# Root and scaling of a gated unit moved ahead of an attention, and an expert layer's gathers split by halves of the features

## What is computed

```
def even_mixer(h_lat, h_ctx, ...):
    ...
    o_lat = window_attention(q_lat, k_lat, v_lat, k_ctx, v_ctx, sink_g, scale)
    s_lat = spatial_gating(z_lat[..., EVEN_CTX_COLS + A_Q_W:], sgu_norm_g, sgu_w, sgu_b)
    y_lat = jnp.concatenate([o_lat, s_lat], axis=-1) @ w_out
    ...

def expert_choice_ffn(h, w_router, w1, w3, w2):
    n_tok, d = h.shape[1], h.shape[2]
    cap = EC_FACTOR * n_tok // N_EXPERTS
    aff = jax.nn.softmax(jnp.einsum('bnd,de->bne', h, w_router).astype(jnp.float32), axis=-1)
    gate, idx = lax.top_k(jnp.swapaxes(aff, 1, 2), cap)
    xs = jax.vmap(lambda hb, ib: hb[ib])(h, idx)
    a = jnp.einsum('becd,edf->becf', xs, w1)
    b = jnp.einsum('becd,edf->becf', xs, w3)
    y = jnp.einsum('becf,efd->becd', jax.nn.silu(a) * b, w2) * gate[..., None].astype(h.dtype)
    ...
```

## Time and profile before

| | us |
|---|---|
| median of 3 runs | 2015.21 |
| lowest, highest | 2009.55, 2015.6 |
| the profiled execution | 2012.53 |
| its span, first to last instruction | 2010.8 |
| PE busy | 1721.9 (86%) |
| DVE busy | 639.9 (32%) |
| ACT busy | 319.0 (16%) |
| HBM read | 580.11 MB |

### The profile page before, as it was taken

The page is one execution under the profiler, slowest core; times in us unless marked ns, Lnnn a source line. Parts: engine busy times, 40 slices in busy tenths (PEclk is TensorE's granted clock), DMA queues, the critical chain, the costliest instruction groups (busy, mean ns, idle before and its releaser), DMA issues.

```text
span 2010.8 us, 23441 instructions
## 1 busy us (share of the span) xinstructions
PE 1721.9 (86%) x10154; PEld 1059.0 (53%) x10154; DVE 639.9 (32%) x1276; ACT 319.0 (16%) x665; POOL 70.7 (4%) x82
## 2 busy tenths in 40 slices
PE   7999999999999998989999878889998765556565
PEld 4557588888888646464433222247577432222223
DVE  2885245688752047131111111121333100000002
ACT  4101231100101125021110000021242100000001
POOL 0000321000000000000000000000140000000000
PEclk8999999999999999989999999999999987887887
DMA  9679324776635022139999999992333999999995
GB/s 408 255 313 386 137 84 172 290 279 264 255 143 230 1 105 120 74 120 394 423 429 428 429 427 427 428 427 110 126 121 141 427 427 426 428 427 427 428 427 227
DMA packets 42437, 582.66 MB, mean 290 GB/s; under 512 B 4704, under 2 KB 4960, under 8 KB 6240
## 3 DMA queue, kind: packets, MB, share of 16 engines
q1 hardware_dynamic: 42336, 581.18, 69.9%
HBM read 580.11 MB, written 1.05 MB: 289 GB/s over the span
## 4 chain that ended last, share of the span: by engine, by line
PE 61%; DMA 30%; DVE 5%; ACT 2%; issue 1%; SPq 0%; DVEq 0%; POOL 0%; ACTq 0%
PE banks L652 38%; DMA ring<-in_experts_dram 29%; PE banks L1272 8%; PE banks L1295 4%; PE banks L1149 3%; PE banks L952 1%; DMA ring<-in_weights_dram 1%; PE banks L637 1%; PE banks L998 1%; PE banks L561 1%; DVE ring L1965 1%; PE banks L1021 1%; DVE small L2415 1%; PE banks L612 0%; PE banks L624 0%
## 5 line engine op out<-in xcount | busy, mean ns | idle before, releaser
L1272 PE MATMUL banks<-ring,arena 128*32 128x256 f32 (+1 forms) x2992 | 389.0, 524 | 164.8 <-DMA ring<-in_experts_dram 161.1
L652 PE MATMUL banks<-hT,ring 128*128 128x256 f32 (+2 forms) x1776 | 405.7, 389 | 6.5 <-ACT hT L1554 5.2
L652 PEld LDWEIGHTS banks<-hT,ring 128*128 128x128 f32 (+1 forms) x1776 | 333.9, 189 | 77.1 <-issue 31.6
L1272 PEld LDWEIGHTS banks<-ring,arena 128*32 128x32 f32 (+1 forms) x2992 | 143.3, 135 | 407.7 <-DMA ring<-in_experts_dram 220.4
L1965 DVE SCALAR_TENSOR_TENSOR ring<-ring,sil_c 128x512 f32<-128x512 f32 x336 | 242.6, 750 | 7.9
L1295 PE MATMUL banks<-ring,arena 128*32 128x256 f32 (+1 forms) x1536 | 186.9, 490 | 61.1 <-DMA ring<-in_experts_dram 38.9
L2617 DVE TENSOR_TENSOR arena<-arena,banks 128x512 f32<-128x512 f32 (+1 forms) x32 | 17.7, 555 | 524.1 <-PE banks L1272 524.1
L1295 PEld LDWEIGHTS banks<-ring,arena 128*32 128x32 f32 (+1 forms) x1536 | 70.0, 126 | 160.4 <-issue 77.4
L652 PE MATMUL banks<-arena,ring 128*128 128x256 f32 (+2 forms) x720 | 151.2, 371 | 2.7 <-POOL arena L2752 1.6
L652 PE MATMUL banks<-ring,hT 128*128 128x512 f32 (+1 forms) x384 | 147.0, 541 | 2.1 <-DVE arena L2174 2.1
L652 PEld LDWEIGHTS banks<-arena,ring 128*128 128x128 f32 (+1 forms) x720 | 130.6, 188 | 23.6 <-issue 2.6
(11 more groups left out here) (322 smaller groups left out, 1203.8 us busy)
## 6 DMA issues: line engine op xcount, KB each, us to landing
ring<-in_experts_dram SPq DMA_DIRECT2D x189, 2048.0 KB, 30.5
ring<-in_weights_dram SPq DMA_DIRECT2D x73, 2048.0 KB, 12.1
ring<-in_weights_dram SPq DMA_DIRECT2D x8, 1408.0 KB, 7.8
arena<-in_experts_dram SPq DMA_DIRECT2D x2, 2048.0 KB, 8.0
ring<-in_weights_dram SPq DMA_DIRECT2D x2, 1152.0 KB, 26.5
cT<-in_ctx_dram SPq DMA_DIRECT2D x2, 1024.0 KB, 7.5
ring<-in_weights_dram SPq DMA_DIRECT2D x2, 1024.0 KB, 15.4
ring<-in_weights_dram SPq DMA_DIRECT2D x1, 1536.0 KB, 28.3
```

What stands on the lines that cost most here:

```text
L652: ins = mm(dst, a, b, start=(i == 0), stop=(i == len(terms) - 1))
L1272: ins = mm(banks[M * q:M * q + M, which, 0:W], xc[:, 4 * half + k, :], w[k][:, W * q:W * q + W], start=(half == 0 and k == 0), stop=(half ...
```

## The change

On ACT the root moves from behind `eu3` to behind `eu0`, into the loop. On DVE `sgu_scaled()` moves from behind tile 2 of the attention to behind `sgu_variance()`, ahead of the attention. In `routed` three token tiles instead of four (layer 0), one instead of two (layer 1), are turned ahead of the affinities. The gather jobs go by a first and by stream second, and those with a = 1 take banks of the second rotation. `experts` waits at its start for the jobs with a = 0 only, and for those with a = 1 ahead of the second half of expert 0's w1.

```diff
--- before.py
+++ after.py
@@ -1167,7 +1167,7 @@
                         ins = mm(o[:, n:n + 17], router_part[s][:, P * c:P * c + P],
                                  const[:, C_RT + 17 * s:C_RT + 17 * s + 17], start=True, stop=True)
                 ins.then_inc(*jobs.fills(job))
-                half = TC * len(streams)
+                half = (3, 1)[l]
                 token_tiles = [(s, c, a) for s in streams for c in range(TC) for a in range(2)]
                 for s, c, a in token_tiles[:half]:
                     tokens_turned(l, s, c, a)
@@ -1181,12 +1181,13 @@
                 if jobs.new(f"mk{l}") > 1:
                     eng.wait_ge(*jobs.is_free(f"mk{l}"))
                 turn(f"mk{l}", [(48 * c, mk[0:48, P * c:P * c + P]) for c in range(TC)]).then_inc(*jobs.fills(f"mk{l}"))
-                for s in streams:
-                    for c in range(TC):
-                        eng.wait_ge(*jobs.is_drained(f"th{l}{s}{c}0"))
-                        eng.wait_ge(*jobs.is_drained(f"th{l}{s}{c}1"))
-                    eng.wait_ge(flag("selection"), sum(len(q) for q in ([0, 1], [0])[:l]) + s + 1)
-                    for a in range(2):
+                for a in range(2):
+                    for s in streams:
+                        if a == 0:
+                            for c in range(TC):
+                                eng.wait_ge(*jobs.is_drained(f"th{l}{s}{c}0"))
+                                eng.wait_ge(*jobs.is_drained(f"th{l}{s}{c}1"))
+                            eng.wait_ge(flag("selection"), sum(len(q) for q in ([0, 1], [0])[:l]) + s + 1)
                         gather_four(l, s, 0, a)
 
             def gather(l, s, half, kk):
@@ -1205,7 +1206,7 @@
             def gather_four(l, s, quarter, a):
 
                 job = f"gq{l}{s}{quarter}{a}"
-                if jobs.new(job, late=(quarter == 1)) > 1:
+                if jobs.new(job, late=(quarter == 1 or a == 1)) > 1:
                     eng.wait_ge(*jobs.is_free(job))
                 o = jobs.bank(job)
                 project([(o[:, P * j:P * j + P],
@@ -1244,8 +1245,7 @@
                 for b in range(4):
                     eng.wait_ge(drained[b], jobs.turns[b])
                 for s in streams:
-                    for a in range(2):
-                        eng.wait_ge(*jobs.is_drained(f"gq{l}{s}0{a}"))
+                    eng.wait_ge(*jobs.is_drained(f"gq{l}{s}00"))
                 for e in range(E):
                     n = E * l + e + 1
 
@@ -1267,6 +1267,9 @@
                     xc = x_slots(l)[:, e]
                     for which in range(2):
                         for half, w in stage_in(which):
+                            if e + which == 0 and half == 1:
+                                for s in streams:
+                                    eng.wait_ge(*jobs.is_drained(f"gq{l}{s}01"))
                             for k in range(4):
                                 for q in range(G):
                                     ins = mm(banks[M * q:M * q + M, which, 0:W], xc[:, 4 * half + k, :],
@@ -1786,9 +1789,10 @@
                 eng.wait_ge(*jobs.is_filled(f"eu{c}"))
                 o = jobs.bank(f"eu{c}")
                 A(e_u[:, c, :], o[:, :], ACT.Gelu_apprx_tanh).then_inc(*act.frees(f"eu{c}"))
-            eng.wait_ge(flag("sgu_var"), 1)
-            eng.wait_ge(*act.last)
-            A(lnst[:, :, 2], lnst[:, :, 2], ACT.Sqrt, scale=1.0 / 512, bias=eps).then_inc(*act.raises("sgu_std"))
+                if c == 0:
+                    eng.wait_ge(flag("sgu_var"), 1)
+                    eng.wait_ge(*act.last)
+                    A(lnst[:, :, 2], lnst[:, :, 2], ACT.Sqrt, scale=1.0 / 512, bias=eps).then_inc(*act.raises("sgu_std"))
             attention("ea", EVEN_TILES, e_p, e_pT, 64.0 ** -0.5, True)
             def routed(l, streams, residuals):
                 ns = len(streams)
@@ -2430,8 +2434,6 @@
                             TT(a[:, 4:6], a[:, 4:6], a[:, 6:8], ALU.add).then_inc(*dve.steps())
                         eng.wait_ge(*dve.last)
                         V.reciprocal(a[:, 0:2], a[:, 4:6]).then_inc(*dve.raises(f"reciprocal_{tag}"))
-                    if tag == "ea" and i == 2:
-                        sgu_scaled()
 
             gains(0, 1, 0, 1, V_M1)
             scale_shift("e1", 0, xT, 1, 0, "h3_0_v")
@@ -2461,6 +2463,7 @@
             for a in range(2):
                 rope_sum(f"esw{a + 1}", e_q[:, 2 * a:2 * a + 2, 0:N], 2, a + 2, "even")
             sgu_variance()
+            sgu_scaled()
             eng.wait_ge(*dve.last)
             TS(neg_sink, sink, -1.0, None, ALU.mult).then_inc(*dve.steps())
             attention("ea", EVEN_TILES, 64.0 ** -0.5,
```

## The result

The kernel after takes **1999.95 us**, the median of 6 executions (1998.51 to 2005.7), beside 2010.76 for the kernel before (6 executions, 2007.88 to 2015.6): ratio 0.9947, 95% interval 0.993 to 0.9963. That is 10.8 us less (7.4 to 14.1 by the interval). Run once more beside other runs of before (median 2011.36) it gave 2000.44 and 0.9943 [0.9927, 0.9959]. The forecast was 2005.0 with a range from 2000.5 to 2010.5: the sign is right, the saving nearly so (9.5 in the sum, 10.8 measured), the forecast time lies 5.05 us above the measured median, and that median lies 0.55 us under the range.

The account below looks back on a forecast made before the run. TensorE carries most of the chain, expert weights' transfers 29%; the first freed slot sets each expert stage's end. Terms 3.4 + 1.7 + 1.8 + 3.1 - 0.5 = 9.5 us: 2003.0 by profile, 2005.7 by median, forecast 2005, range 2000.5 to 2010.5.

Parts of the forecast that it names:

- part 1: Gated unit: root hidden on ACT, scaling moved off DVE between attention tiles 2 and 3; 3.4 us gain, bounds 2.4 to 5.8.
- part 4: Layer 1's routing: both gather jobs share bank 6, so the second waits; 0.5 us loss, bounds -2.8 to +2.8.
- A: Rival: the clock gives nothing back in layer 0, saving 6.4 us, time 2006 to 2009; chance 0.20.
- B: Rival: layer 1's bank collision costs its full 2.8 us, attention gives only 2.4; 2008 to 2011; chance 0.14.
- Rival D: Slower: even attention's tiles 5 to 15 run at half clock, over about 22 us; up to 2022; chance 0.03.
- the prediction's 0: Gated unit on ACT: moving the root and its table loads gains 0 and costs 0, being hidden.
- Part 2: Layer 0's routing: three token tiles ahead of the affinities start these earlier; 1.7 us gain, bounds 0.8 to 1.7.
- Part 3: Layer 0's gathers by halves: the hole ahead of expert 0 goes; 1.8 us gain, bounds 1.5 to 1.8.
- The clock of layer 0's gathers: TensorE's hole before layer 0's gathers halves to 1.5 us, so they run at full clock; 3.1 us gain, bounds 0 to 3.1.
- C: Rival: something else holds tile 3, the split wait doesn't bind, only tile order acts, 1.7 us; 2011 to 2015; chance 0.09.
- The fixed distance: Both layers' expert stages end a fixed distance behind the first freed weight slot, so whatever precedes it counts in full.

Follow-up runs that it names:

- experiment 5: Kernel before with only ScalarE's root moved behind the first Gelu, VectorE's scaling left in place: 2010.76 us, ratio 1.0001.
- experiments 1 to 3: Kernel before with one piece each: gated unit's root and scaling 2004.03 us; token-tile order 2007.96; gathers by halves with late banks and split wait 2008.3.
- experiment 7: Kernel before plus unread identity products on TensorE ahead of the chosen slots, 6 in layer 0 and 11 in layer 1: 2009.49 us, ratio 0.9994.
- experiment 8: Kernel after, layer 1's second gather on its own bank, plus 8 idle products between halves of expert 0's first projection in both layers: 1998.38 us, ratio 0.9947.
- experiment 9: Kernel after run again unchanged, in more rounds: 2000.44 us, ratio 0.9943 against the kernel before.
- experiment 11: Kernel after, layer 1's second gather on its own bank, plus idle products ahead of both layers' chosen slots and the odd attention's output sums: 1992.79 us, ratio 0.9908.
- experiment 10: Kernel after with layer 1's second gather job on bank 7 instead of bank 6: 1998.17 us, ratio 0.9932 against the kernel before.

## Why the prediction was right or wrong, point by point

- **The step that failed is the last one, from the sum to the forecast.** The sum was 9.5 us against the profiled 2012.53, 2003.0. I then went up by 2.0, to 2005, because the median of three executions lay 2.7 above the profiled one, at 2015.2. Over the 78 executions of the kernel before that ran beside the experiments the median is 2011.4 (2004.1 to 2019.7), so the time of the profiled execution was nearly ordinary (its clock, 0.946 where the 78 have 0.951 in the mean, was not), and two of the three were high ones. The correction had the wrong sign. Of the 5.05 us between 2005 and 1999.95, 2.0 are this correction, 1.8 the place of the profiled 2012.53 above the 2010.76 of before in the comparison, and 1.3 the sum itself (9.5 where 10.8 were measured). Sum against this level: 2001.9, measured 1999.95 and 2000.44.
- **The range was too narrow below** for the same reason: I let it end at 2000.5, above 2003.0 less what the bounds of the single terms allowed (up to 2.4 more for part 1 alone, 3.3 more for part 4). The text gave it as holding the forecast, A and most of B; it made no room for the high side of the terms.
- **Part 1**, term 3.4, bounds 2.4 to 5.8. The mechanism is right in each point: ScalarE's side 0 (experiment 5), VectorE's 3.46. What follows at tiles 4 and 5 brought more: over the whole attention the eight kernels with both moves have 86.46 to 87.63, mean 87.0, and the five with the scaling at its old place (before, 2, 3, 5, 7) 91.09 to 91.84, mean 91.3. So 4.3 is the size, 5.4 between the two first profiles, and the 3.4 was mis-sized by 0.9: with the scaling gone the attention was also granted the full clock more often (half clock for 0 to 3.4 us in the eight, 3.4 to 10.2 in the five). Rival D, which had it at half clock for more than 22 us, fell.
- **On the table loads** the Trainium skill ("ScalarE: Activation LUTs", section What ACT_TABLE_LOAD costs) puts 1283 ns and a drain of some 1380 ns to every switch to a different set of functions. The rows of after show the load of 1.28, but the root starts 0.04 us behind it, and two switches with the root take 2.92 us where by the Trainium skill the switches alone would take 5.3 (an estimate from its two figures). The measurement decides, and with it the prediction's 0.
- **Part 2**, term 1.7, bounds 0.8 to 1.7: 1.2 by the means and 0.7 to 1.0 at equal clock, so the term belonged at the lower end of its bounds. The 4.0 between the two first profiles is this and the luck of the clock.
- **Part 3**, term 1.8: about 1.9 in every kernel with the split. As forecast.
- **The clock of layer 0's gathers**, term 3.1 ("I take it whole"): the argument fell. Without added products the gathers lasted 10.24, 7.38, 9.01, 9.01 and 7.38 with the old order (mean 8.6), and 9.01, 9.01 and five times 7.38 with the new (mean 7.85). That is 0.8 in the mean, and not certain with so few. I had taken the one profile of before for the rule, when it was the worst of five, and I had derived from the length of one hole what the clock would do. The hole was wrong too: it is 2.2 to 2.3 us in every kernel with the new order, not 1.5, because the fourth token tile now stands behind the affinities, which I had left out when I let the tiles end where they did.
- **Part 4**, term -0.5, bounds -2.8 to +2.8: the double use of bank 6, its stop (1.46, forecast 1.4) and who ends it (VectorE) came as said; -0.2 in the mean, -0.7 in the first pair. The distance was 7.95, forecast 6.4 to 8.2. Rival B's form of it, a full price of 2.8, did not come. The other bound was mis-sized: by the prediction's own times a full clock would give back 7.23 less 1.8, 1.36, 0.1 and 1.8, that is 2.2 and not 2.8. The Trainium skill ("TensorE: Matmul & The Clock Gate", section A second HAM failure mode: psum-queue depth-cycling) has short stops between groups on banks make the clock swing; here the stretch with the stop ran at 0.50, but so did it before without one, so no run here shows that the stop did it.
- **Rivals A and C.** A, that the clock gives nothing back in layer 0's gathers, came closer than the forecast's term on that one point (0.8 of 3.1), but its time of 2006 to 2009 was too high: it had 6.4 us in all where 10.8 were measured, and it carried the same correction of 2.7. C fell with experiments 1 to 3.
- **The fixed distance** held in layer 1 (437.8 to 440.0) and was put on the wrong ground in layer 0 (experiment 8), without harm to the sum.

By means the terms are 4.3 + 1.2 + 1.9 + 0.8 - 0.2 = 8.0 us; measured are 10.8 and 10.9. The sum is inside the interval (7.4 to 14.1). That the recorded 9.5 came nearer is luck: it had the gathers' clock 2.3 too high and part 2 0.5 too high, and part 1 0.9 too low, and some 2.8 us of the measured saving are in no part. **What stays open:** whether the change also makes half clock rarer elsewhere. The mean clock of the 12 executions of after and experiment 9 is 0.9521, of the 78 of before 0.9506; by the line in the last section that would be some 1.3 us of the 2.8 (an estimate), but with so few executions it is no clear difference. The three parts alone gave 0.35, 0.16 and 0.26%, together 15.4 us, 4.6 more than the whole, but with 2.5 to 3 us of uncertainty each, this doesn't contradict a plain sum.

## What to carry to other kernels

Take the step that is worth something from the engine that is late (here VectorE between two attention tiles), and ask of every edit which partner it needs: root and scaling were worth 0 apart and 3.5 to 4.3 together. When jobs are added to a rotation of buffers, count where the next user lands: a layer further down two jobs met in one bank and 2 us of that stage's gain were lost, and one line brought them back. Make a forecast against the profiled execution with the spread of executions as its width, not shifted by a median of three, and give a clock seen low in one execution only part of its price.

## What the runs showed of the hardware that I had not expected

- Two executions of the same instructions differ by 5.9 us in span (1997.4 and 2003.3), 4.4 of it in one stage, with a mean granted clock of 1.00 against 0.94 in the same window of it. Over the 78 executions of before the mean clock of an execution and its time go together: by a straight line 0.9 us less for each 0.001 of clock (correlation -0.73).
- Idle products on TensorE cost nothing where it waits anyway (from MAX8 to the gathers of layer 0 it takes 6.74 to 6.76 us in all fourteen profiles, with them and without), and they may buy clock: layer 1's gathers took 3.81 in place of 5.2 to 5.4 in both kernels that had them, and the median of experiment 11 is 5.4 us under that of experiment 10, with intervals that touch. In layer 0 the same measure did nothing in experiment 7, so each place has to be tried.
- A table load on ScalarE of 1.28 us is followed by its ACTIVATE within 0.04 us.
